# Moving the modulation weights, reordering the first loads and spreading the last adding DMAs in a one-core transformer pass

## Chip, cores and metric

One core of one Trainium2 chip. The metric is the time of one execution on the device in microseconds (us), a median over executions. The kernel before took 3865.44 us (two runs, 3865.24 to 3865.64).

## What is computed

One layer over 1152 tokens (128 of context, 1024 of samples) of width 1024, cut here to what the change touches:

```python
mod = silu(cond) @ w_mod + b_mod            # shift1, scale1, gate1, shift2, scale2, gate2, each 1024 wide
h   = x * (1 + scale1) + shift1             # context and sample tokens have each their own mod
z   = h @ w_in                              # 1024 -> 1728 columns
# mixer A: gelu, standardize, 128x128 spatial gate; mixer B: latent attention with 128 cached keys
x   = LN1(alpha * x + gate1 * (concat(A, B) @ w_o))
h2  = x * (1 + scale2) + shift2
# PEER: 8 heads x 16 experts of 16384 per token, by top-k of product keys
x   = LN2(alpha * x + gate2 * sum_k g_k * gelu(h2 . u[e_k]) * v[e_k])
```

## The kernel before, in words

Tokens are nine tiles of 128, tile 0 the context. Four blocks run one after the other; each ends when all engines have come to its end.

1. **mixer_inputs** (L149). First the shift1 and scale1 of both conditions: the table `w_mod` is read in 16 pieces of 128x1024 into four buffers in `free` (SP, L222), and TensorE takes each 128x128 piece as the stationary operand and two columns of `silu` as the moving one (L486: 16 pieces x 8 = 128 matmuls; an f32 matmul stands in the trace as two records). VectorE adds the bias (L325) and 1 (L328, `mod_ready`). The weights `w_in`, `w_s`, ... come by ScalarE's DMA queue (L380 to L384), and one semaphore, `wl`, stands for them all. GpSimd then zeroes the 25 MB table `g_cells` in 32 writes (L243), once `mod_ready` is there. Then, tile by tile: ScalarE makes the modulated rows (`mod_h`, L338) from `xt`, TensorE projects (`project`, L430) and does the rest of the tile (`finish`, L439 to L473), VectorE does `dve_tile`, ScalarE `act_tile` (gelu L345, evictions L361 to L373). `finish(i)` comes after `project(i+1)`; `mod_h(i+2)` stands in `act_tile(i)` ahead of the eviction L361 that frees TensorE for the transposes L468. `xt` is one buffer, loaded by SP at L225; the rotation table `rot` is one buffer too, loaded at L227. SP's order is: wait until `xt` has been read, load rows i, wait until the queries of tile i-1 are rotated (`qr_ready`), load table i.
2. **middle** (L506). Attention, output product, first LayerNorm, routing. Here shift2, scale2 and the gates are made in the other way: `silu` is the stationary operand (two columns of weights), a 128x512 piece of the table moves (`mod`, L715), the 2x512 result is copied to a row buffer `mrow` whose third row is the bias, and small matmuls against `sel` turn the row to columns (L727). For three of the sample tiles (3, 4, 5 are `DENSE[0]`; 0, 1, 2 are `DENSE[1]`; 6, 7, 8 `STILES`) the experts' weights go to dense tables. For `DENSE[1]` GpSimd adds them to `g_cells` by indirect DMAs of 128 cells, one for each of 128 (head, expert) columns and each of three tiles: 384 of them (`place`, L142), in 24 groups of 16. Groups of one tile are ordered by a wait at the head of each (L139). 20 of the 24 groups stand in this block.
3. **weigh** (L1201). TensorE, VectorE and ScalarE build the table `g_blocks` for `DENSE[0]`, SP stores it (L1230), and GpSimd issues the last 4 groups, 64 adding DMAs (L1239).
4. **experts** (L1347), the sweep. All 128 tiles of 128 experts are passed over twice (g = 0 to 255), first for `DENSE[0]`, then for `DENSE[1]`. TensorE does `hidden(g+2)` (L1511) and `down(g)` (L1525) in each step; SP loads `uw` (L1432) and `vw` (L1426) and every fourth step `gw`. Beside it GpSimd gathers rows for `STILES` (L1476, 384 gathers of 1 MB, two in four of five steps, into a ring of six, each after the VectorE sum `v_done` that frees its place), and VectorE does the dot products (L1613) and the sums (L1630). The second pass reads `g_cells` and waits for all adding DMAs; at g = 112 SP waits for those of the last tile too, as it overwrites `slots`.

Of the kernel before, what the change touches and what calls it, by code (L numbers as in the profile page):

```python
# [22 lines left out]
P = 128  # L23
# [77 lines left out]
def build(nc, a):  # L101
# [11 lines left out]
    with es:  # L113
# [10 lines left out]
        with ExitStack() as mid:  # L124
# [4 lines left out]
            mixer_inputs(nc, a, sb, sem, PS, ident, modc, sp1, silu, slots, krT, kT, vv, g_dram)  # L129
            placed = [sem(f"g_placed{d}") for d in range(CT)]  # L130
            middle(nc, a, sb, sem, PS, ident, modc, sp1, silu, slots, krT, kT, vv, x1_dram, gate_dram, g_dram, placed)
        weigh(nc, a, sb, sem, PS, ident, slots, g_dram, placed)
# [16 lines left out]
def mixer_inputs(nc, a, sb, sem, PS, ident, modc, sp1, silu, slots, krT, kT, vv, g_dram):  # L149

    with ExitStack() as c:
# [34 lines left out]
        NJ, NW = 2 * DK, 4  # L186
        free = sb(c, "free", [P, NW * D])
        bmod = sb(c, "bmod", [P, NJ])
        flat = slots[:, :, :].rearrange("p n c -> p (n c)")
        wm = free[:, 0:NW * D].rearrange("p (w k c) -> p w k c", w=NW, k=DK)  # L190
        hT1 = free[:, 0:D].rearrange("p (k t) -> p k t", k=DK)
        hs = [hT[:, :, :], hT1]
        zero = free[:, 2 * D:2 * D + ZW]
# [4 lines left out]
        ml = [sem(f"a_m{k}") for k in range(NW)]  # L198
        silu_ready, m_used, m_made, mod_ready, id0, id1 = (sem(f"a_{n}") for n in (
            "silu", "mused", "mmade", "mod", "id0", "id1"))  # L200
        xl, rl = sem("a_x"), sem("a_rot")
# [8 lines left out]
        nw = 12  # L210

        with nc.Block() as block:
            @block.sync
            def _(sp):
                sp.dma_start(cond[:, :, :], a["cond"]).then_inc(cl, 16)
                sp.dma_start(bmod[:, :], a["b_mod"]).then_inc(cl, 16)
                sp.dma_start(xt[:, :, :], a["xT"][0, :, :, :]).then_inc(xl, 16)
                sp.dma_start(rot[:, :, :], a["rot"][0, :, :, :]).then_inc(rl, 16)
                with sp.Fori(0, NJ // NW) as j:
                    for k in range(NW):  # L220
                        sp.wait_ge(m_used, j * NW + k + 1)
                        sp.dma_start(wm[:, k, :, :], a["w_mod"][j * NW + k, :, :, :]).then_inc(ml[k], 16)  # L222
# [98 lines left out]
            def _(dve):  # L321
                dve.wait_ge(cl, 32)
# [1467 lines left out]
```

## Time and profile before

| | |
|---|---|
| median of the runs | 3865.44 us |
| the profiled execution, own time | 3864.64 us |
| its span in the trace | 3862.8 us |
| mixer_inputs | 0 to 520.5 us |
| middle | 520.5 to 1459.3 us |
| weigh | 1459.3 to 1666.0 us |
| experts | 1666.0 us to the end |
| DVE busy, share of the span | 68% |
| ACT, POOL busy | 33%, 35% |

The trace gives each engine's instructions with start and length, and for idle time before them what ended it. PE is TensorE's matmul side, PEld its weight loads, DVE VectorE, ACT ScalarE, POOL GpSimd, SP the engine that issues most DMAs; "SPq" is an instruction in its queue. A row "[9.85 <-ACT ...]" says that the engine stood idle for 9.85 us until that instruction. In windows, PEclk is the granted clock as a share of 2.4 GHz, and the DMA share is the mean busy share of the 16 DMA engines.

### The profile page before, as it was taken

Reading aid. Unit: us, or ns where it says so; the run is one execution under the profiler, and the core shown is the slowest. Engines: PE = TensorE matmul, PEld = TensorE weight load, DVE = VectorE, ACT = ScalarE, POOL = GpSimd, SP = SyncE. Lnnn points to the kernel's source line nnn. Section 1 sums busy time; section 2 is a strip of 40 time slices with the busy share of each in tenths; the row PEclk is TensorE's granted clock in tenths of the full one; section 3 lists DMA queues with packets and bytes.
Section 4 is the critical chain, followed back from the end, with each engine's and each line's share of the span. In section 5 each row is a group of like instructions: output and inputs, shape, how many; then the busy total and the mean of one; then the engine's idle time right before and its main releaser. Section 6 shows DMA issues by size and latency. Waiting matters only on the chain.

```text
span 3862.8 us, 47329 instructions
## 1 busy us (share of the span) xinstructions
PE 3453.0 (89%) x17472; PEld 2853.2 (74%) x17472; DVE 2639.6 (68%) x5338; ACT 1273.8 (33%) x2399; POOL 1350.3 (35%) x828
## 2 busy tenths in 40 slices
PE   7877789999999976469999999999999999999996
PEld 6444434666666665459999999998888999999996
DVE  0111111566666699558888888888999888888866
ACT  0122222222322327523333333333333333333332
POOL 0100000078888847932322322332233223222302
PEclk9888889999999998879999999999999999999998
DMA  6500043355555544479999999999889998999953
GB/s 241 229 12 12 12 171 146 144 145 146 147 147 146 147 149 131 131 273 353 348 354 361 338 361 356 346 361 348 338 344 341 358 356 341 358 360 341 356 203 117
DMA packets 268027, 952.87 MB, mean 247 GB/s; under 512 B 74520, under 2 KB 125848, under 8 KB 208928
## 3 DMA queue, kind: packets, MB, share of 16 engines
q1 hardware_dynamic: 150720, 511.85, 36.0%
q0 software_dynamic: 115200, 428.07, 32.1%
q10 hardware_dynamic: 1888, 10.06, 0.6%
q8 instruction: 134, 2.20, 0.2%
q14 instruction: 85, 0.70, 0.1%
HBM read 888.70 MB, written 61.18 MB: 246 GB/s over the span
## 4 chain that ended last, share of the span: by engine, by line
PE 51%; DVE 4%; DMA 1%; issue 1%; ACT 0%; POOLq 0%; POOL 0%; SPq 0%; ACTq 0%; DVEq 0%
PE bank L1511 26%; PE bank L1525 25%; DMA vw<-in_v 1%; DVE ring L1613 1%; DVE accS L1630 1%; DVE uL L1691 1%; DVE vL L1686 0%; DVE slots L1668 0%; ACT vR L1576 0%; DVE st L1659 0%; DVE ga L1706 0%; DVE cL L1683 0%; DVE slots L1642 0%; DVE slots L1656 0%; DVE hL L1605 0%
## 5 line engine op out<-in xcount | busy, mean ns | idle before, releaser
L1476 POOL DMA_INDIRECT ring<-in_uv,slots x384 | 591.0, 1539 | 1396.9 <-DVE accS L1630 1301.0
L142 POOL DMA_INDIRECT g_cells<-slots x384 | 689.6, 1796 | 390.8 <-DVE slots L1178 263.8
L1511 PE MATMUL bank<-hR,uR 128*128 128x384 f32 x2048 | 692.1, 338 | 89.5 <-DVE uL L1691 89.5
L1511 PE MATMUL bank<-hR,uL 128*128 128x384 f32 x2048 | 691.6, 338 | 0.0
L1511 PE MATMUL bank<-hL,uR 128*128 128x384 f32 x2048 | 690.1, 337 | 0.0
L1630 DVE SCALAR_TENSOR_TENSOR accS<-ring,cs,accS 128x1024 f32<-128x1024 f32 x381 | 489.6, 1285 | 13.6
L1525 PE MATMUL bank<-vR,cR 128*128 128x512 f32 x1536 | 477.5, 392 | 0.7 <-DVE slots L1642 0.7
L1525 PE MATMUL bank<-vR,cL 128*128 128x512 f32 x1536 | 476.0, 391 | 0.0
L1525 PE MATMUL bank<-vL,cR 128*128 128x512 f32 x1536 | 475.7, 391 | 0.0
L1511 PEld LDWEIGHTS bank<-hR,uR 128*128 128x128 f32 x2048 | 388.0, 189 | 102.2 <-DVE uL L1691 92.6
L1613 DVE CUSTOM_DVE_ANT_0 ring<-ring,slots 128x1024 f32<-128x1024 f32 x384 | 460.2, 1236 | 0.1
L1570 ACT ACTIVATE cR<-ga 128x384 fp32r<-128x384 f32 x256 | 134.5, 525 | 924.9 <-PE bank L1525 829.1
L1511 PEld LDWEIGHTS bank<-hL,uR 128*128 128x128 f32 x2048 | 387.8, 189 | 9.6
L1511 PEld LDWEIGHTS bank<-hR,uL 128*128 128x128 f32 x2048 | 387.4, 189 | 0.0
L1686 DVE TENSOR_TENSOR vL<-vw,vR 128x1024 fp32r<-128x1024 f32 x256 | 319.9, 1250 | 60.3 <-ACT vR L1576 59.5
L1525 PEld LDWEIGHTS bank<-vL,cR 128*128 128x128 f32 x1536 | 288.3, 188 | 64.4
L1525 PEld LDWEIGHTS bank<-vR,cL 128*128 128x128 f32 x1536 | 288.2, 188 | 62.8
L1525 PEld LDWEIGHTS bank<-vR,cR 128*128 128x128 f32 x1536 | 284.7, 188 | 44.2 <-issue 1.0
L1691 DVE TENSOR_TENSOR uL<-uw,uR 128x1024 fp32r<-128x1024 f32 x256 | 311.9, 1218 | 5.6 <-ACT uR L1584 5.6
L1576 ACT ACTIVATE vR<-vw 128x1024 fp32r<-128x1024 f32 x256 | 267.7, 1046 | 18.5 <-DMA vw<-in_v 18.5
L771 PE MATMUL bank<-slots,wr 128*128 128x128 f32 x2304 | 264.2, 276 | 8.0 <-ACT slots L909 6.7
L1584 ACT ACTIVATE uR<-uw 128x1024 fp32r<-128x1024 f32 x256 | 267.6, 1045 | 6.3 <-DMA uw<-in_u 6.3
(226 smaller groups left out, 4048.3 us busy)
## 6 DMA issues: line engine op xcount, KB each, us to landing
uw<-in_u SPq DMA_DIRECT2D x256, 512.0 KB, 6.0
vw<-in_v SPq DMA_DIRECT2D x256, 512.0 KB, 6.9
wr<-in_w_pq SPq DMA_DIRECT2D x36, 2048.0 KB
wr<-in_w_o SPq DMA_DIRECT2D x18, 2048.0 KB
g_cells<-free POOLq DMA_DIRECT2D x32, 768.0 KB, 7.7
g_blocks<-stage SPq DMA_DIRECT2D x12, 2048.0 KB, 6.5
gw<-g_blocks SPq DMA_DIRECT2D x32, 768.0 KB, 13.8
gw<-g_cells SPq DMA_DIRECT2D x32, 768.0 KB, 8.8
```

The source lines that it names most:

```text
L142: pool.indirect_dma_start(out=g_dram[1][:, :], out_offset=bass.IndirectOffsetOnAxis(ap=slots[:, i, D + k:D + k + 1].bitcast(U32), axis=0), ...
L771: mm = pe.matmul(ps[:, l * P:(l + 1) * P], w[:, at:at + P], slots[:, i, k * P:(k + 1) * P], start=(k == 0), stop=(k == DK - 1))
L1476: pool.indirect_dma_start(out=ring[:, k % R, :], out_offset=None, in_=a["uv"], in_offset=bass.IndirectOffsetOnAxis(ap=ids[:, k // P, k % P ...
L1511: mm = pe.matmul(A[t][:, 0:CW], w[:, t, k, :], h[:, k, :], start=(k == 0 and w is uR and h is hR), stop=(k == DK - 1 and w is uL))
L1525: mm = pe.matmul(ACC[2 * tt + half][:, :], w[:, t, tt * P:(tt + 1) * P], v[:, t, half * 512:(half + 1) * 512], start=(m == 0 and w is cR a ...
L1570: act.activation(cR[:, x % 2, :], ga[:, x % 2, :], ACT.Copy).then_inc(c_r, 1)
L1576: act.activation(vR[:, x % 2, :], vw[:, x % 2, :], ACT.Copy).then_inc(v_r, 1)
L1584: act.activation(uR[:, x % 2, :, :], uw[:, x % 2, :, :], ACT.Copy).then_inc(u_r, 1)
L1613: dve.tensor_tensor_reduce(out=ring[:, k % R, 0:D], in0=ring[:, k % R, 0:D], in1=whole(STILES[k // P]), scale=1.0, scalar=0.0, op0=ALU.mul ...
L1630: dve.scalar_tensor_tensor(accS[:, t, :], ring[:, k % R, D:2 * D], one, accS[:, t, :], ALU.mult, ALU.add).then_inc(v_done, 1)
L1686: dve.tensor_tensor(vL[:, x % 2, :], vw[:, x % 2, :], vR[:, x % 2, :].bitcast(F32), ALU.subtract).then_inc(v_l, 1)
L1691: dve.tensor_tensor(uL[:, x % 2, :, :], uw[:, x % 2, :, :], uR[:, x % 2, :, :].bitcast(F32), ALU.subtract).then_inc(u_l, 1)
```

## The change

Four edits.

- **Modulation by moving weights.** shift1 and scale1 are now made as the block middle makes the rest: four pieces of 128x4096 (`wm`, lying in `big` and `slots`, which are free then), `silu` stationary with two columns, 4 x 8 matmuls of 512 columns, copy of each 2x512 row by VectorE, small matmuls against `sel_a` into columns.
- **First loads in one queue.** All first loads are issued by SP, in the order of use; ScalarE issues none. `w_in` comes in the four column groups of the projection, each with its semaphore (`zl`), the cached keys' weights have theirs (`kl`), the rest is waited for only ahead of `finish(0)`. Rows of tile 1 go straight into `hT1`, and are modulated in place.
- **Rows ahead of the rotation table.** SP's loop loads rows i, then waits for the queries of tile i-2 and loads table i-1.
- **Last adding DMAs in the sweep.** `place` takes a part of a group; the last 64 adding DMAs leave `weigh` and stand in `experts`, one in each of the steps g = 0 to 63, behind the step's gathers.

```diff
@@ place
-def place(pool, slots, g_dram, placed, d, h):
+def place(pool, slots, g_dram, placed, d, h, first=0, last=TOPK):
-    if h:
+    if h and first == 0:
         pool.wait_ge(placed[d], h * TOPK * 16)
-    for k in range(h * TOPK, (h + 1) * TOPK):
+    for k in range(h * TOPK + first, h * TOPK + last):
@@ mixer_inputs, sync
+                for ch in range(NM):
+                    sp.dma_start(wm[ch], a["w_mod"][ch, :, :]).then_inc(ml[ch], 16)
                 sp.dma_start(xt[:, :, :], a["xT"][0, :, :, :]).then_inc(xl, 16)
+                sp.dma_start(hT1, a["xT"][1, :, :, :]).then_inc(x1l, 16)
...
+                for n, (at, w) in enumerate(Z):
+                    sp.dma_start(w_in[:, :, at:at + w], a["w_in"][:, :, at:at + w]).then_inc(zl[n], 16)
...
-                with sp.Fori(1, NT) as i:
+                with sp.Fori(2, NT) as i:
                     sp.wait_ge(h_ready, i)
                     sp.dma_start(xt[:, :, :], a["xT"][i, :, :, :]).then_inc(xl, 16)
-                    sp.wait_ge(qr_ready, i)
-                    sp.dma_start(rot[:, :, :], a["rot"][i, :, :, :]).then_inc(rl, 16)
+                    sp.wait_ge(qr_ready, i - 1)
+                    sp.dma_start(rot[:, :, :], a["rot"][i - 1, :, :, :]).then_inc(rl, 16)
+                sp.wait_ge(qr_ready, NT - 1)
+                sp.dma_start(rot[:, :, :], a["rot"][NT - 1, :, :, :]).then_inc(rl, 16)
@@ mixer_inputs, tensor
+                def columns(ch):
+                    pe.wait_ge(m_row, ch + 1)
+                    for k in range(4):
+                        at = 8 * ch + 2 * k
+                        mm = pe.matmul(PS[7][:, at:at + 2], mrow[0:3, ch, k * P:(k + 1) * P], sel[:, :],
+                                       start=True, stop=True)
+                    mm.then_inc(m_cols, 1)
+
+                for ch in range(NM):
+                    pe.wait_ge(ml[ch], 16)
+                    for k in range(DK):
+                        mm = pe.matmul(PS[ch][0:2, :], silu[:, k, :], wm[ch][:, k * 512:(k + 1) * 512],
+                                       start=(k == 0), stop=(k == DK - 1))
+                    mm.then_inc(m_used, 1)
+                    if ch:
+                        columns(ch - 1)
+                columns(NM - 1)
+                pe.wait_ge(kl, 48)
                 pe.wait_ge(mod_ready, 1)
@@ weigh, gpsimd
-                for d, h in GROUPS[EARLY:]:
-                    place(pool, slots, g_dram, placed, d, h)
@@ experts, gpsimd
+                late = GROUPS[EARLY:]
...
+                    if g // TOPK < len(late):
+                        place(pool, slots, g_dram, placed, *late[g // TOPK], g % TOPK, g % TOPK + 1)
```

SP's queue at the start of mixer_inputs, before (the loop at L219 runs four times, the one at L223 eight times):

```order
L215 DMA cond<-in_cond 128x16
L216 DMA bmod<-in_b_mod 128x16
L217 DMA xt<-in_xT 128x1024
L218 DMA rot<-in_rot 128x128
...
L225 ISA [waits a_h]
L225 DMA xt<-in_xT 128x1024
L227 ISA [waits a_qr]
L227 DMA rot<-in_rot 128x128
```

And now (the loop at L234 runs seven times):

```order
L217 DMA cond<-in_cond 128x16
L218 DMA free<-in_b_mod 1x2048
L220 DMA big<-in_w_mod 128x4096 x2
L220 DMA slots<-in_w_mod 128x4096 x2
L221 DMA xt<-in_xT 128x1024
L222 DMA free<-in_xT 128x1024
L224 DMA w_kn<-in_w_kn 128x1024
L224 DMA cckT<-in_cckT 128x256
L224 DMA w_v<-in_w_v 128x1024
L226 DMA w_in<-in_w_in 128x8x512 x2
L226 DMA w_in<-in_w_in 128x8x384
L226 DMA w_in<-in_w_in 128x8x320
```

The pair of row load and table load looks alike in both loops; what has moved is the number of the tile that the table's wait (`a_qr`) asks for, one less than before against the rows loaded beside it, so that rows i no longer stand behind the rotated queries of tile i-2. The first loads stand in one line, the modulation table ahead of everything large.

GpSimd at the end of weigh and the start of the sweep, before (`ring` is the gathers' buffer, `g_cells` the table that the adding DMAs write):

```order
L1236 IOTA iob 128x128
L142 DMA g_cells<-slots 6291456x1 x64
L1224 UNCONDITIONAL_BRANCH
L1471 UNCONDITIONAL_BRANCH
L1476 DMA ring<-in_uv,slots 128x2048 x216
```

And now:

```order
L1260 IOTA iob 128x128
L1248 UNCONDITIONAL_BRANCH
L1493 UNCONDITIONAL_BRANCH
L1498 DMA ring<-in_uv,slots 128x2048 x8
L142 DMA g_cells<-slots 6291456x1 x2
L1498 DMA ring<-in_uv,slots 128x2048 x2
L142 DMA g_cells<-slots 6291456x1
L1498 DMA ring<-in_uv,slots 128x2048 x2
L142 DMA g_cells<-slots 6291456x1
```

The 64 adding DMAs have left the block weigh; eight gathers come first, then one or two adding DMAs between pairs of gathers.

## Rows read from the trace of the kernel before

**Rows 1.** The page's first part: busy time by engine, share of the span.

```profile
PE 3453.0 (89%) x17472; PEld 2853.2 (74%) x17472; DVE 2639.6 (68%) x5338; ACT 1273.8 (33%) x2399; POOL 1350.3 (35%) x828
```

**Rows 2.** Waits of PE in 120 to 500 us: total us, times, longest.

```profile
PE bank L468 <- ACT slots L361: 70.8, 7, 12.2
PE bank L430 <- ACT u L345: 20.1, 7, 4.5
```

**Rows 3.** Timeline of the start: start us, us, engine, line, operation.

```profile
26.93 54.77 PE L486 MATMUL bank<-silu,free 128*128 128x2 f32 x256 [26.93 <-DMA free<-in_w_mod]
...
82.04 0.17 DVE L328 TENSOR_SCALAR sp<-modc 128x16 f32<-128x16 f32 x1
```

**Rows 4.** Timeline: end of tile 0, projection, end of tile 1, projection.

```profile
143.06 1.46 PE L463 MATMUL bank<-w_qr,qlT 128*128 128x256 f32 x6
...
157.62 0.63 PE L473 MATMUL bank<-ident,qr 128*128 128x128 f32 x2
...
162.80 26.38 PE L430 MATMUL bank<-w_in,hT 128*128 128x512 f32 x64 [4.55 <-ACT u L345]
...
197.61 1.46 PE L463 MATMUL bank<-w_qr,qlT 128*128 128x256 f32 x6
...
201.78 0.33 SPq L225 DMA_DIRECT2D xt<-in_xT  x1
...
208.92 1.11 PE L468 MATMUL bank<-ident,u 128*128 128x128 f32 x4 [9.85 <-ACT slots L361]
...
209.83 0.63 PE L473 MATMUL bank<-ident,qr 128*128 128x128 f32 x2
...
213.09 25.12 PE L430 MATMUL bank<-w_in,free 128*128 128x512 f32 x64 [2.62 <-ACT u L345]
```

**Rows 5.** Timeline of PE: end of tile 7, which has no rows to wait for.

```profile
494.65 1.46 PE L463 MATMUL bank<-w_qr,qlT 128*128 128x256 f32 x6
495.95 0.60 PE L468 MATMUL bank<-ident,u 128*128 128x128 f32 x4
497.87 0.44 PE L473 MATMUL bank<-ident,qr 128*128 128x128 f32 x2 [1.32 <-DVE qr L318]
```

**Rows 6.** Windows: stretch, us, busy by engine, PEclk, DMA share, GB/s.

```profile
95.00:145.00 50.00, 48.92 (x177) 28.96 (x175) 6.97 (x30) 8.24 (x17) 13.29 (x25) 1.00 1.01 408
499.00:500.00 1.00, 0.00 (x0) 0.00 (x0) 0.00 (x0) 1.00 (x1) 0.00 (x0) 0.90 0.20 58
530.00:535.00 5.00, 5.00 (x9) 0.77 (x7) 0.00 (x0) 0.00 (x0) 0.00 (x0) 0.61 1.00 418
1611.00:1631.00 20.00, 0.00 (x0) 0.00 (x0) 0.00 (x0) 0.00 (x0) 16.07 (x11) 0.50 0.23 0
1700.00:2100.00 400.00, 400.00 (x2026) 364.31 (x2025) 351.64 (x464) 143.75 (x232) 116.86 (x76) 1.00 0.94 352
```

**Rows 7.** Timeline of the block middle's start: moving weights and their load.

```profile
520.50 0.34 SPq L644 DMA_DIRECT2D wr<-in_w_mod  x1
...
528.15 16.75 PE L715 MATMUL bank<-wr,silu 128*2 128x512 f32 x32 [3.73 <-DMA wr<-in_w_mod]
...
565.61 1.05 PE L727 MATMUL bank<-sel,s 3*128 3x2 f32 x8
...
568.04 7.03 PE L715 MATMUL bank<-wr,silu 128*2 128x512 f32 x16
```

**Rows 8.** Timeline in the second half of weigh: the 33rd of its 64 adding DMAs.

```profile
1545.76 56.59 POOL L142 DMA_INDIRECT g_cells<-slots  x1 [5.28 <-DMA g_cells<-slots]
```

**Rows 9.** Waits of SP in 1600 to 1850 us: total us, times, longest.

```profile
SPq L1224 <- PEq L1224: 55.4, 1, 55.4
```

**Rows 10.** The sweep: a gather, a later dot product (timelines); line L1476, 1700:2100, landing.

```profile
1711.50 1.86 POOL L1476 DMA_INDIRECT ring<-in_uv,slots  x1 [12.34 <-DVE accS L1630]
...
1729.55 1.22 DVE L1613 CUSTOM_DVE_ANT_0 ring<-ring,slots 128x1024 f32<-128x1024 f32 x1
...
DMA to landing us min/median/max: 6.5/9.5/12.2
```

More of the change, by code:

```diff
@@ L184, in mixer_inputs @@
         rs = sb(c, "rs", [P, G + 2])
-        NJ, NW = 2 * DK, 4
-        free = sb(c, "free", [P, NW * D])
-        bmod = sb(c, "bmod", [P, NJ])
+        NJ, NM = 2 * DK, 4
+        free = sb(c, "free", [P, 3 * D])
+        sel = sb(c, "sel_a", [3, 2])
         flat = slots[:, :, :].rearrange("p n c -> p (n c)")
-        wm = free[:, 0:NW * D].rearrange("p (w k c) -> p w k c", w=NW, k=DK)
+        wm = [tile[:, k * DK * 512:(k + 1) * DK * 512] for tile in (big, flat) for k in range(2)]
         hT1 = free[:, 0:D].rearrange("p (k t) -> p k t", k=DK)
+        mrow = free[0:3, D:3 * D].rearrange("p (c d) -> p c d", c=NM)
         hs = [hT[:, :, :], hT1]
-        zero = free[:, 2 * D:2 * D + ZW]
+        zero = free[:, D:D + ZW]
         zeroed = [sem(f"a_zero{k}") for k in range(4)]
@@ L197, in mixer_inputs @@
         cl, wl = sem("a_small"), sem("a_weights")
[L198 to L201, printed above, removed]
+        ml = [sem(f"a_m{k}") for k in range(NM)]
+        kl, zl = sem("a_kv"), [sem(f"a_in{n}") for n in range(len(Z))]
+        silu_ready, m_used, m_row, m_cols, m_made, mod_ready, sel_ready, id0, id1 = (sem(f"a_{n}") for n in (
+            "silu", "mused", "mrow", "mcols", "mmade", "mod", "sel", "id0", "id1"))
+        xl, x1l, rl = sem("a_x"), sem("a_xone"), sem("a_rot")
         h_ready, z_ready = sem("a_h"), sem("a_z")
@@ L377, in _ @@
             def _(act):
-                for dst, src in ((w_in, "w_in"), (w_s, "w_s"), (w_qn, "w_qn"), (w_qr, "w_qr"),
-                                 (w_kn, "w_kn"), (w_v, "w_v"), (cckT, "cckT")):
-                    act.dma_start(dst[:, :, :], a[src]).then_inc(wl, 16)
-                for dst, src in ((b_s, "b_s"), (g_q, "g_q"), (g_kv, "g_kv")):
-                    act.dma_start(dst[:, :], a[src]).then_inc(wl, 16)
-                for half in range(2):
-                    act.dma_start(krT[half * ROPE:(half + 1) * ROPE, P:2 * P], a["ckrT"]).then_inc(wl, 16)
                 act.wait_ge(cl, 32)
@@ L387, in _ @@
                 act.wait_ge(mod_ready, 1)
-                mod_h(act, 0, 0, 0)
-                mod_h(act, 1, 1, 1)
+                mod_h(act, 0, 0, 0, first=True)
+                act.wait_ge(x1l, 16)
+                mod_h(act, 1, 1, 1, src=hT1)
                 act.wait_ge(k_mm, 1)
@@ L428, in project @@
                         pe.wait_ge(lat_ready, i)
+                    if first:
+                        pe.wait_ge(zl[n], 16)
                     for k in range(DK):
@@ L492, in _ @@
                 values(pe, cckT)
-                project(pe, 0, 0)
+                project(pe, 0, 0, first=True)
                 project(pe, 1, 1)
+                pe.wait_ge(wl, nw * 16)
                 finish(pe, 0)
```

63 lines of the change are left out of this document (31 added, 32 removed).

## Prediction

> **What bounds the kernel now.** I read the page first. TensorE is busy for 89% of the span [rows 1], so what it does not do is 410 us, and a change that leaves its long stages alone can win only what stands in those gaps or what TensorE does needlessly. I then went through the gaps stage by stage.
>
> In the sweep there is nothing to win for a change that leaves its matmuls alone: in a stretch of 400 us TensorE is busy for 400 [rows 6]. The waits of TensorE in mixer_inputs name one cause: seven times, 70.8 us in all, it stands ahead of the transposes L468 until ScalarE has done the eviction L361 [rows 2]. The timeline says why. SP issues the rows at 201.78, behind the rotation of tile 1's queries, and ScalarE, which has the modulation of those rows ahead of its eviction, lets TensorE go on at 208.92 [rows 4]. Tile 7, whose ScalarE program has no modulation, has no such wait [rows 5]. Third, the start: TensorE waits until 26.93 and then needs 54.77 us for 256 records of two columns; the modulation is ready at 82.2 [rows 3]. Fourth, the end of weigh: SP has seen its last store land and then stands 55.4 us at the block's end [rows 9], with only GpSimd at work: its 33rd adding DMA had taken 56.59 us, to 1602.35 [rows 8], and 31 were still to come.
>
> **The start.** Removed: the 16 small pieces, and the wait behind ScalarE's loads. Added: four pieces of 2 MB, 32 matmuls of 512 columns. The block middle does just this. Its first piece is issued at 520.50 and TensorE starts on it at 528.15, 7.65 us later; a piece costs 7.03 us for 16 records [rows 7]. Here the first piece is issued behind two small loads, at about 1.7, so TensorE starts at 9.3. Next pieces come each 2.1 MB / 418 GB/s = 5.0 us later, the rate of SP's queue alone [rows 6], so TensorE is the slower one. Turning a row to columns costs 1.05 us for 8 records [rows 7], four times. 9.3 + 4 x 7.0 + 4 x 1.05 = 41.5, less some overlap of starts (each record group's length holds its pipeline fill), plus VectorE's copy and add, some 0.4: I take 41 for mod_ready against 82.2. Gain **41**. If TensorE starts at half its clock, as in the block middle (32 records in 16.75 us where two times 7.03 would be 14.06 [rows 7]), it is 38; if the copies to rows are all hidden and the first piece comes sooner, 44.
>
> The projection needs `w_in` by then. Ahead of it in the queue are 10.6 MB, at 418 GB/s landed at 28; `w_in`'s 7.1 MB take 17 more, 45. Its first part is needed at about 47 and its last at 66. Even at half that rate the last would come at 64. So this costs nothing, though the zeroing now begins while loads are under way. That zeroing fills the DMA engines (408 GB/s, share 1.01, for its whole length [rows 6]); it will end near 112, while tile 0's work ends near 106, and there ScalarE waits for two small stores. I put 2 us on that; 0 to 6 are possible.
>
> **The rows.** Rows i are now issued one tile earlier, and have some 45 us to land. What comes late next? Tile 7 shows it: from the start of L463 to the end of L473 it takes 498.31 - 494.65 = 3.66 us, with a new wait of 1.32 for VectorE's rotation [rows 5]; tile 1 takes 210.46 - 197.61 = 12.85 [rows 4]. Six tiles: the waits are 70.8 - 12.2 = 58.6 [rows 2], less 6 x 1.32, plus 6 x 0.7 for transposes that then run at the full clock (1.11 and 0.63 against 0.60 and 0.44 [rows 4, 5]): 54.9. Tile 0: 143.06 to 158.25 is 15.2 [rows 4]; its queries are copied, not rotated, so I leave it 2.5: 12.7, less the 2 for stores. Gain **65.6**. The wait of the next projection for ScalarE's gelu, 2.62 in tile 1, stays.
>
> **The clock.** The projection behind each gap takes 25.12 us in tile 1 [rows 4]; behind tile 0 it takes 26.38. By the 7.03 us that 8 x 512 columns take [rows 7], its 8 x 1728 would take 23.7. The rest is a start at 1.2 GHz after TensorE's pause. Will that go? In tile 7 the clock falls inside 499 to 500 [rows 6], 3.3 us after L468's end, although L473 ran between. The new gap from L468 to the projection is 1.32 + 0.44 + 2.6 = 4.4 us, as long as that. So the clock will fall in part of the tiles. Bounds: nothing, and 7 times the mean of 1.4 and 2.7 = 14. I take somewhat under 1 a tile, **6**, in the middle.
>
> **The adding DMAs.** With GpSimd out of weigh the 55.4 us of SP's wait go [rows 9], but for the engines' meeting itself; gain **55**. The work of weigh doesn't change. In the sweep each of steps 0 to 63 gets one more DMA on GpSimd. GpSimd is busy there for 116.86 of 400 us [rows 6], and 64 adds at some 1.5 (16.07 / 11 [rows 6]) to 2.4 us find room behind the gathers. On the DMA engines ten to eleven of them alone make a share of 0.23 in 20 us [rows 6]: 0.43 us of all sixteen each, or 5% of a step of the sweep, on top of 0.94 (a step is 42 records, 24 of L1511 and 18 of L1525, so the 2026 records of those 400 us [rows 6] are 48 steps of 8.3 us). That is close to full. Bounds: nothing, and 64 x 0.43 = 27 us if each pushes a load that TensorE waits for. TensorE waits for none in that stretch now, so I take **3** lost.
>
> By the Trainium skill (SBUF — State Buffer, Who interferes with whom) a VectorE instruction with two SBUF inputs contends with a GpSimd instruction that reads SBUF, and the second to issue is blocked until the first ends. The one 56.59 us instruction [rows 8] stands beside a VectorE that has such instructions back to back, and lasts much longer than any one of them; so the rule's direction agrees and its length doesn't.
>
> **Sum.** 41 + 65.6 + 6 + 55 - 3 = 164.6. The profiled execution took 3864.64 (span 3862.8 and 1.8 around it), 0.8 under the median: 3864.6 - 164.6 = **3700**.
>
> **Rivals.**
> - *The adding DMAs are held in the sweep, as one was in weigh.* VectorE is busy for 351.64 of 400 us [rows 6], so it pauses for 5 of the 41.5 us of five steps, mostly in the fifth, which has no dot products. An add that is held to that pause holds the gathers behind it, since GpSimd takes them in order. A gather is issued at 1711.50 for a dot product at 1729.55 and needs 9.5 to land [rows 10]: 8.5 us of slack. An add that is held through three steps (about 23 us) costs VectorE 14.5; in 64 / 5 = 12.8 such runs that is 185 us: 3700 + 185 = **3885**, slower than before. It decides from a net loss of 165 / 12.8 = 13 us in each run. Against it: in that stretch 76 instructions of GpSimd keep to 116.86 us, 1.54 each [rows 6], and they are of the same kind.
> - *A DMA-bound first pass.* The whole 27 us above, and loads that jitter more: **3725 to 3735**. For it: share 0.94 already.
> - *The rows come no earlier, or TensorE's wait only moves to another instruction of ScalarE.* Then the 65.6 and the 6 stay: **3771**. Against it: tile 7's row.
> - *The clock stays up in all tiles.* 8 us more on the clock, and 4 at the start if it is up there too: **3688**.
>
> **Chances.** Forecast 0.62; clock stays up 0.14; DMA-bound 0.14; rows no earlier, or weigh's end held by something else, 0.07; adds held 0.03. The forecast's own range is 3688 to 3714 (start -3/+3, stores -2/+4, clock -8/+6, sweep -3/+7, added as if independent and rounded up). To hold 8 in 10 I go to 3684 and 3728. A measurement tells about 2%, 77 us, from no change: the forecast is at 4.3%, so faster 0.95; the case of held adds, whole or in part, mostly lies within 2%: same 0.04, slower 0.01.
>
> **What would show it.** Right: mod_ready near 41; mixer_inputs ends near 408 to 416 instead of 520; no wait for an eviction ahead of the transposes; the sweep starts about 10 us after VectorE ends weigh; the first pass keeps steps of 8.31 us. Wrong: an adding DMA in the sweep over 5 us with dot products waiting for `ring`; TensorE waiting for VectorE's `uL` or `vL` in steps 0 to 63; waits for `zl` in tile 0; gelu L345 of tile 1 waiting much over 2 us for the small stores. The prediction as a whole is wrong if the sweep is longer by over 25 us than 2197, or the mixers' gain is under 90.

## The result, and the profile after

The changed kernel takes 3718.27 us (3717.35 to 3719.2) against 3865.44: ratio 0.9619, 95% interval 0.9578 to 0.9661. Run again beside the experiments it took 3716.55 (3716.06 to 3718.13), ratio 0.9616 (0.96 to 0.9632). The forecast was 3700, range 3684 to 3728: the sign and the range hold, and the sum is 18 us too favourable.

I first put the two profiled executions side by side by block, since that tells which terms to look at.

| stage | before, us | after, us | difference | forecast |
|---|---|---|---|---|
| start, to `mod_ready` | 82.2 | 44.1 | -38.1 | -41 |
| rest of mixer_inputs | 438.3 | 380.4 | -57.9 | -71.6 |
| middle | 938.8 | 938.6 | -0.2 | 0 |
| weigh | 206.7 | 151.0 | -55.7 | -55 |
| experts | 2196.8 | 2203.3 | +6.5 | +3 |
| span | 3862.8 | 3717.4 | -145.4 | -164.6 |

The page's first part, against [rows 1]. TensorE's busy time falls by 22 us (for the most part the two columns' matmuls), GpSimd's by 46 (the one long adding DMA).

```profile
PE 3430.8 (92%) x17312; PEld 2805.9 (75%) x17312; DVE 2640.8 (71%) x5343; ACT 1277.7 (34%) x2399; POOL 1304.7 (35%) x828
```

**The start**, a timeline as in [rows 3]. TensorE starts at 9.44 instead of 26.93. Its first 32 records take 16.48 us, where two times 7.03 [rows 7] would be 14.06; the last rows are the modulation's columns, VectorE's copy, and the add that is `mod_ready`. SP stands 30.20 us at its own issues of `w_in`, with nothing urgent behind.

```profile
6.28 30.20 SPq L226 DMA_DIRECT2D w_in<-in_w_in  x4
...
9.44 16.48 PE L506 MATMUL bank<-big,silu 128*2 128x512 f32 x32 [9.44 <-DMA big<-in_w_mod]
...
41.73 1.94 PE L499 MATMUL bank<-sel_a,free 3*128 3x2 f32 x16
...
43.70 0.19 DVE L342 COPY modc<-bank 128x32 f32<-128x32 f32 x1 [1.19 <-PE bank L499]
43.93 0.17 DVE L344 TENSOR_SCALAR sp<-modc 128x16 f32<-128x16 f32 x1
```

**The tiles**, TensorE's waits from 90 to 424 us, against [rows 2]. The 70.8 us for the eviction are gone. In their place stand eight waits of 1.32 for the rotated queries, as tile 7 had foretold [rows 5], and one for gelu is now 12.3 long.

```profile
PE bank L443 <- ACT u L362: 27.7, 7, 12.3
PE bank L486 <- DVE qr L331: 10.6, 8, 1.3
```

The timeline around that one wait, and the next two projections. ScalarE issues the two small stores of tile 0 and stands 9.90 us until they have landed; its gelu, and with it TensorE's projection of tile 2, come behind. The projections take 25.8 and 26.2 us, where [rows 4] has 26.38 and 25.12.

```profile
106.95 0.39 ACTq L409 DMA_DIRECT2D out_new_ckv<-ckv  x1
107.37 1.25 ACTq L410 DMA_DIRECT2D out_new_krope<-kr  x1
117.23 1.28 ACT L362 ACT_TABLE_LOAD   x1 [9.90 <-DMA out_new_krope<-kr]
...
119.18 25.80 PE L443 MATMUL bank<-w_in,hT 128*128 128x512 f32 x64 [12.27 <-ACT u L362]
...
159.63 26.04 PE L443 MATMUL bank<-w_in,free 128*128 128x512 f32 x64 [2.57 <-ACT u L362]
200.33 26.18 PE L443 MATMUL bank<-w_in,hT 128*128 128x512 f32 x64 [2.58 <-ACT u L362]
```

The windows (columns as in [rows 6]) say why the stores are slow: to 112 us the DMA engines are full, by the zeroing.

```profile
106.00:112.00 6.00, 0.83 (x6) 0.35 (x4) 0.41 (x1) 0.90 (x2) 0.53 (x1) 0.85 1.03 410
112.00:114.00 2.00, 0.00 (x0) 0.00 (x0) 0.00 (x0) 0.00 (x0) 0.00 (x0) 0.50 0.96 282
```

**The end of weigh.** SP's wait of 55.4 us [rows 9] is 0.2.

```profile
SPq L1248 <- PEq L1248: 0.2, 1, 0.2
```

**The adds in the sweep**, the answer for line L142 (ns: shortest, median, longest), and a window of 400 us among them, against the last of [rows 6]. No add is held for long. GpSimd's busy time goes from 116.86 to 215.83 us, the DMA share from 0.94 to 0.97, and TensorE does not notice: 400.00 of 400.

```profile
L142 POOL DMA_INDIRECT g_cells<-slots x64: 1607/1978/2416, 1549.0 to 2070.8; - x64
```

```profile
1550.00:1950.00 400.00, 400.00 (x2024) 364.17 (x2023) 351.83 (x465) 144.60 (x232) 215.83 (x125) 1.00 0.97 352
```

Of the 19 us that the sum is too favourable, 13.7 are missing in the tiles, in two terms (the rows and the clock); the start is 2.9 short, and the sweep has lost 6.5 us at a place still to be found.

### The profile page after: what moved, and what is told of

Read it like the earlier page. It is cut to its first block, busy times and chain, and to the rows that moved or that the text cites. A ratio compares the mean times of both kernels' runs of the same rounds, so it can differ in the third digit from the quotient of the medians.

```text
span 3717.4 us, 46918 instructions
## 1 busy us (share of the span) xinstructions
PE 3430.8 (92%) x17312; PEld 2805.9 (75%) x17312; DVE 2640.8 (71%) x5343; ACT 1277.7 (34%) x2399; POOL 1304.7 (35%) x828
## 4 chain that ended last, share of the span: by engine, by line
PE 51%; DVE 5%; DMA 2%; issue 1%; ACT 0%; SPq 0%; POOLq 0%; POOL 0%; ACTq 0%; DVEq 0%
PE bank L1536 26%; PE bank L1550 25%; DMA vw<-in_v 2%; DVE ring L1638 1%; DVE accS L1655 1%; DVE uL L1716 1%; DVE vL L1711 1%; DVE cL L1708 0%; DVE ga L1731 0%; DVE slots L1693 0%; ACT vR L1601 0%; DVE slots L1667 0%; DVE st L1684 0%; DVE slots L1681 0%; DVE hL L1630 0%
## 5 line engine op out<-in xcount | busy, mean ns | idle before, releaser
L142 POOL DMA_INDIRECT g_cells<-slots x384 | 642.9, 1674 | 386.3 <-DVE slots L1202 263.9
L1550 PEld LDWEIGHTS bank<-vR,cR 128*128 128x128 f32 x1536 | 284.7, 188 | 44.1 <-issue 0.9
L1708 DVE TENSOR_TENSOR cL<-ga,cR 128x384 fp32r<-128x384 f32 x256 | 149.5, 584 | 171.3 <-ACT cR L1595 122.5
```

The lines of the kernel that those rows point to most:

```text
L142: pool.indirect_dma_start(out=g_dram[1][:, :], out_offset=bass.IndirectOffsetOnAxis(ap=slots[:, i, D + k:D + k + 1].bitcast(U32), axis=0), ...
L1550: mm = pe.matmul(ACC[2 * tt + half][:, :], w[:, t, tt * P:(tt + 1) * P], v[:, t, half * 512:(half + 1) * 512], start=(m == 0 and w is cR a ...
L1708: dve.tensor_tensor(cL[:, x % 2, :], ga[:, x % 2, :], cR[:, x % 2, :].bitcast(F32), ALU.subtract).then_inc(c_l, 1)
```

## The experiments

Every kernel is timed against the one before on the same chip. That one took 3865.56 us beside the first four kernels, 3867.92 beside the four of the store stall, the clock and ScalarE's loads ahead of its silu, and 3867.15 beside the other four. A difference of two kernels from different groups is therefore known to about 2.5 us only; where it is small, the blocks' starts in the profiles are given too. The four that leave a part of the change out, or do it alone, come first, then the misses.

### The change again

> The changed kernel, once more. If the sweep's 6.5 us over before (2203.3 against 2196.8 us, with three loads of vw that took 12 to 24 us near step 112 where before had one) belong to the change, this profile has them again, with the sweep at 2203 +/- 1 and the time at 3718. If they are the chance of one execution, the sweep lies between 2196 and 2204 and the times spread by some us.

Measured: 3716.55 (3716.06 to 3718.13). The gain is a property of the two programs, and the experiments below are set against both figures of the change, 3716.55 and 3718.27.

### Only the adding DMAs moved

```diff
@@ before: place, weigh, experts as in the change; mixer_inputs untouched
```

> Before, with the adding DMAs of weigh in the sweep and nothing else. Theory (weigh was held by GpSimd alone, the sweep hides the adds): weigh 151 us instead of 206.7, first pass with steps of 8.31 us, so 3865 - 55 + 0 to 6 = 3810 to 3816. Rival (the adds are what makes the sweep 6.5 us longer): 3816, with TensorE's late steps near step 112 as in the changed kernel. If the sweep is 2197 here, the 6.5 us come from elsewhere and it is 3810.

Measured: 3810.72 (3808.02 to 3812.04), ratio 0.9857 (0.984 to 0.9873): 54.8 us gained, where the forecast had 55 less 3. The waits of TensorE ahead of the transposes stay (69.3 us). The longest of its 64 adds in the sweep takes 2.60 us.

### The change without that part

```diff
@@ weigh, gpsimd
+                for d, h in GROUPS[EARLY:]:
+                    place(pool, slots, g_dram, placed, d, h)
@@ experts, gpsimd
-                    if g // TOPK < len(late):
-                        place(pool, slots, g_dram, placed, *late[g // TOPK], g % TOPK, g % TOPK + 1)
```

> The changed kernel with the 64 adding DMAs back in weigh. Theory: +50 to +56 us, 3768 to 3774. In before one add there took 56.6 us beside a VectorE that paused nowhere. If such a hold is a matter of chance in the order of the two engines, weigh is shorter here or has its hold elsewhere: 64 adds at 2.7 us apiece end after 175 us, so weigh could be 175 to 207 us and the time 3742 to 3774. If it is fixed by the program, weigh is 206.7 again.

Measured: 3774.29 (3770.51 to 3775.85), ratio 0.9762: 57.7 us are given back. The long add is there again, and SP's wait with it, as in [rows 8] and [rows 9]:

```profile
1450.44 56.63 POOL L142 DMA_INDIRECT g_cells<-slots  x1 [5.25 <-DMA g_cells<-slots]
```

```profile
SPq L1248 <- PEq L1248: 55.3, 1, 55.3
```

56.63 against 56.59: what holds it belongs to the program at that place, not to the chance of one execution. Both traces also show what the hold ends with. Here is VectorE's last instruction of weigh in the kernel before, and then in this one with the add that follows the long one:

```profile
1600.39 0.54 DVE L1342 TENSOR_TENSOR cb<-e,wf 128x384 f32<-128x384 bf16 x1
```

```profile
1505.07 0.58 DVE L1366 TENSOR_TENSOR cb<-e,wf 128x384 f32<-128x384 bf16 x1
...
1507.37 1.54 POOL L142 DMA_INDIRECT g_cells<-slots  x1 [0.30 <-issue]
```

VectorE ran without a pause beside the long add, up to 1600.93 and 1505.65; the add ended at 1602.35 and 1507.07, 1.42 us later both times, which is nearly the length of an add beside an idle VectorE (1.54). So the add seems to have got hardly anywhere until VectorE stopped. Most of the adds shortly ahead of it took 2.43 beside the same VectorE work. That VectorE holds it is argued from these rows; no kernel changed VectorE's work there, and why the 33rd is held and the 32nd is not stays open (the 33rd is the first in this block behind a wait of GpSimd for its own DMAs, 5.28 and 5.25 us). Moving the adds took them away from that place.

### The change with the rows in their old place

```diff
@@ mixer_inputs, sync
+                sp.wait_ge(qr_ready, 1)
+                sp.dma_start(rot[:, :, :], a["rot"][1, :, :, :]).then_inc(rl, 16)
                 with sp.Fori(2, NT) as i:
                     sp.wait_ge(h_ready, i)
                     sp.dma_start(xt[:, :, :], a["xT"][i, :, :, :]).then_inc(xl, 16)
-                    sp.wait_ge(qr_ready, i - 1)
-                    sp.dma_start(rot[:, :, :], a["rot"][i - 1, :, :, :]).then_inc(rl, 16)
-                sp.wait_ge(qr_ready, NT - 1)
-                sp.dma_start(rot[:, :, :], a["rot"][NT - 1, :, :, :]).then_inc(rl, 16)
+                    sp.wait_ge(qr_ready, i)
+                    sp.dma_start(rot[:, :, :], a["rot"][i, :, :, :]).then_inc(rl, 16)
```

> The changed kernel with SP's old order (rows i behind the rotated queries of tile i-1). Theory: TensorE waits again ahead of the transposes in tiles 0 to 6, 9.8 us each less the 1.3 us that stand there now, 6 x 8.5 + 8 to 11 for tile 0; the stall for the small stores in tile 0 is partly the same time, so +52 to +62: 3770 to 3780. Rival (the clock's behaviour gives some of it back): the projections start at the half clock in both orders, so this adds under 3 us either way.

Measured: 3773.53 (3772.06 to 3775.28), ratio 0.9761: the order of two DMAs on SP is worth 57 us. Its waits of TensorE from 90 to 480 us are those of [rows 2] again:

```profile
PE bank L481 <- ACT slots L378: 71.4, 7, 13.2
```

### The first modulation with weights at rest, in the new queue

The changed kernel, with the 16 pieces as stationary operand as before (128 matmuls, bias added by VectorE), from the four new loads.

```diff
@@ mixer_inputs, tensor
-                    for k in range(DK):
-                        mm = pe.matmul(PS[ch][0:2, :], silu[:, k, :], wm[ch][:, k * 512:(k + 1) * 512],
-                                       start=(k == 0), stop=(k == DK - 1))
+                    for q in range(4):
+                        for k in range(DK):
+                            mm = pe.matmul(acc[:, 4 * ch + q, :], wm[ch][:, k * 512 + q * P:k * 512 + (q + 1) * P],
+                                           silu[:, k, :], start=(k == 0), stop=(k == DK - 1))
```

> The changed kernel with the first modulation by weights that stay in the array and two columns that move, as before (128 matmuls in 16 pieces, bias added by VectorE), but with the one queue and its order kept. Theory A (moving the weights is worth what TensorE spends on the form: 54.8 us before against 30.6 here): TensorE from 9.4 to about 64 us, mod_ready at 64 to 66 us against 44.1, the projections' weights are there by then, so the first tile goes by 20 us later and all after it: 3733 to 3740. Theory B (the form was paced by its loads in two queues, and with one queue the weights at rest take about as long as moving ones): 3714 to 3722. The old 54.8 us had no stated wait inside, so I take A, 3737.

Measured: 3735.77 (3734.42 to 3736.88), ratio 0.966. TensorE starts at 9.5 and `mod_ready` is at 64.79 (its row: 64.62, 0.17 long), 20.7 us later than in the changed kernel; the time is 17.5 to 19.2 longer. Theory A. So of the start's 38.1 us about 20 belong to the form of the matmul and the rest, 17.5 (26.93 less 9.44), to the loads: their order, their queues and the size of the pieces (2 MB here too, 0.5 MB before). The next two ask about the queues.

### Two queues, ScalarE's loads ahead of its silu

```diff
@@ mixer_inputs: the loads of w_kn, cckT, w_v, w_in, b_s, ... ckrT move from sync to scalar
             def _(act):
+                for dst, src in ((w_kn, "w_kn"), (cckT, "cckT"), (w_v, "w_v")):
+                    act.dma_start(dst[:, :, :], a[src]).then_inc(kl, 16)
+                for n, (at, w) in enumerate(Z):
+                    act.dma_start(w_in[:, :, at:at + w], a["w_in"][:, :, at:at + w]).then_inc(zl[n], 16)
...
                 act.wait_ge(cl, 32)
                 act.activation(silu[:, :, :], cond[:, :, :], ACT.Silu).then_inc(silu_ready, 1)
```

> The changed kernel with the weights' first loads issued by ScalarE again, ahead of its silu, beside SP's queue. Theory: ScalarE is held by its queue and makes silu near 21 us or later, and the modulation's pieces share the DMA engines with 8 MB of other weights; mod_ready near 22.5 + 4 x 7 + 4 = 54 to 58 instead of 44, so +10 to +14 us, 3728 to 3732. Then the single queue is worth 10 to 14 of the 38 us at the start and the moving weights the rest. Rival (the single queue is what matters): +25 us or more.

Measured: 3755.08 (3749.36 to 3759.72), ratio 0.9703: 37 to 39 us lost, three times what was expected. By its figure this is the rival's case (the single queue is what matters), but the cause is narrower than that. The timeline of ScalarE shows a thing that I had not priced. Its queue stands 33.93 us at the four issues of `w_in`, and the silu waits behind them:

```profile
2.18 33.93 ACTq L388 DMA_DIRECT2D w_in<-in_w_in  x4
36.14 4.07 ACTq L390 DMA_DIRECT2D b_s<-in_b_s  x1
...
45.64 0.21 ACT L396 ACTIVATE silu<-cond 128x16 f32<-128x16 f32 x1
```

### Two queues, the silu first

The same, with the two lines of the silu ahead of the loads.

> The changed kernel, with the weights' loads issued by ScalarE as in the run with two queues (3755.1), but behind its silu instead of ahead of it. Theory A (what cost 37 us there is that ScalarE stood at its own DMA issues, 33.9 us at w_in, with the silu behind them): the silu is done by 10 us, TensorE starts at 9 to 12 us, and what is left is that w_mod shares the DMA engines: at half of 408 GB/s its four chunks of 2 MB land about 10 us apart instead of 5, TensorE's 30.6 us stretch to at most 45, mod_ready between 44 and 58 us, time 3716 to 3732. Theory B (the sharing of the DMA engines is what costs, wherever the silu stands): the last chunk of w_mod lands at 65 us or later, mod_ready near 80 as in the run before, time 3745 to 3758.

Measured: 3720.08 (3716.68 to 3725.41), ratio 0.9625 (0.9609 to 0.9641), which includes the changed kernel's 0.9616. Theory A at its favourable end: ScalarE stands as long, with nothing that TensorE needs behind it yet, and the sharing of the DMA engines costs 0.2 us at `mod_ready` (44.32 against 44.10).

```profile
2.98 0.21 ACT L386 ACTIVATE silu<-cond 128x16 f32<-128x16 f32 x1 [0.95 <-DMA free<-in_b_mod]
...
4.57 32.25 ACTq L390 DMA_DIRECT2D w_in<-in_w_in  x4
```

```profile
44.15 0.17 DVE L334 TENSOR_SCALAR sp<-modc 128x16 f32<-128x16 f32 x1
```

This also reads the kernel before anew. There, too, ScalarE's silu stood behind its loads, as its timeline shows: 12.35 us at one small issue, and the silu only at 22.38. TensorE's first row there names the DMA of `w_mod` at 26.93 [rows 3], the last of the things it waited for; that load shared the DMA engines with the weights. So there both were late, and which would have been enough alone no kernel tried.

```profile
6.07 12.35 ACTq L382 DMA_DIRECT2D g_kv<-in_g_kv  x1
...
22.38 0.21 ACT L386 ACTIVATE silu<-cond 128x16 f32<-128x16 f32 x1
```

The Trainium skill (Trainium Kernel Development and Optimization, Key Constraints) says that issuing from several engines saves no more than issue time, as all transfers share the same DMA engines. The run with the silu first agrees (44.32 against 44.10), and the one with the silu behind shows that the issue time is not small on an engine that has something else to do.

### The store stall: waited for later

ScalarE waits for the two stores ahead of tile 1's square root instead of ahead of its gelu.

```diff
@@ mixer_inputs, scalar
                 act.wait_ge(var_ready, i + 1)
+                if not first:
+                    act.wait_ge(stored, 32)
                 act.activation(sd[:, :], var[:, :], ACT.Sqrt).then_inc(sd_ready, 1)
...
                 act.dma_start(a["new_krope"], kr[:, 0, :]).then_inc(stored, 16)
-                act.wait_ge(stored, 32)
```

> The changed kernel, where ScalarE waits for the two small stores of tile 0 only ahead of tile 1's root (which lets VectorE overwrite their source), not ahead of tile 1's gelu. Theory (the projection of tile 2 waits 12.3 us because ScalarE stands for 9.9 us on these stores): that wait falls to 2.6, -9 to -10 us, 3708 to 3709. Rival (TensorE waits for something else as well): under -4 us.

Measured: 3712.29 (3710.24 to 3713.59), ratio 0.9597 (0.9581 to 0.9613): 4.3 us better. The longest wait of the projections is 3.9 instead of 12.3, while ScalarE now stands 6.02 us ahead of the square root. In the profiles the block middle begins at 417.3 us, against 424.5 and 423.4 in the two of the changed kernel, so 6.1 to 7.2 of the 8.4 come through in the tiles. The medians show less, and they come from two groups (6.6 us if each is set against its own kernel before). The 9 to 10 expected were too much either way.

### The store stall: zeroing behind the stores

```diff
@@ mixer_inputs, gpsimd
-                pool.wait_ge(mod_ready, 1)
+                pool.wait_ge(stored, 32)
                 pool.memset(zero, 0.0).then_inc(zero_set, 1)
```

> The changed kernel, where GpSimd zeroes g_cells only after the two small stores have landed. Theory (the stores are slow because the zeroing fills the DMA engines, and the changed kernel starts it 38 us earlier against less work ahead of the stores): they land in 2 to 3 us as in before, the wait of the projection falls from 12.3 to 4.6, -7 to -8 us, 3710 to 3711; nothing later needs the table before 740 us. If the stores are slow for another reason, 3718.

Measured: 3711.0 (3710.63 to 3713.13), ratio 0.9595 (0.9579 to 0.9611): 5.5 us better. ScalarE's stand falls from 9.90 to 4.01 and the projection's wait to 6.38, and the block middle begins 5.4 to 6.5 us earlier:

```profile
111.50 1.28 ACT L362 ACT_TABLE_LOAD   x1 [4.01 <-DMA out_new_krope<-kr]
...
113.45 25.42 PE L443 MATMUL bank<-w_in,hT 128*128 128x512 f32 x64 [6.38 <-ACT u L362]
```

With nothing but the time of the zeroing changed, the stores land 5.9 us sooner, so the zeroing is the cause of these 5.9 us. It is not the whole stall. In the kernel before, ScalarE stood only 2.12 us for the same two stores. In the changed kernel and in this one SP issues the next rows beside them (at 107.44 and 107.61); the DMA share from 108 to 110 us is 0.91 here, where the kernel before had 0.27 in the two microseconds behind its stores. No kernel moved these rows.

### The clock kept up

TensorE multiplies `ident` by `w_kn` in its pauses, into a bank whose content has been read by then; these results are unused.

```diff
@@ mixer_inputs, finish
                 mm.then_inc(tra, 1)
+                pe.wait_ge(v_ev, i + 2)
+                pe.matmul(PS[6][:, :], ident[:, :], w_kn[:, 0, :], start=True, stop=True)
+                pe.matmul(PS[6][:, 0:P], ident[:, :], w_kn[:, 0, 0:P], start=True, stop=True)
                 pe.wait_ge(qr_ready, i + 1)
...
                 mm.then_inc(trq, 1)
+                for w in (512, 512, 256):
+                    pe.matmul(PS[6][:, 0:w], ident[:, :], w_kn[:, 0, 0:w], start=True, stop=True)
```

> The changed kernel with five extra matmuls per tile, whose results nobody reads, in TensorE's two pauses at the end of a tile (640 columns in the first, 1280 in the second). Theory (each projection takes 26.2 us instead of 23.4 because the clock falls in those 4.4 us): clock at its upper level through the projections of tiles 3 to 8, 2.8 us less each, minus up to 0.5 us where the extra matmuls overrun: -14 to -17 us, 3701 to 3704. Rival (the projection is slow for its reads or waits): no gain or +3 us.

Measured: 3703.05 (3699.47 to 3710.75), ratio 0.957 (0.9554 to 0.9586): 13.5 us better. The profiled execution is the longest of the four. First the windows of the changed kernel at the pause between tile 1's end and the projection of tile 3 behind it, then those of this one:

```profile
158.00:159.00 1.00, 0.00 (x0) 0.00 (x0) 0.00 (x0) 0.99 (x2) 0.00 (x0) 0.52 0.49 142
161.00:163.00 2.00, 2.00 (x3) 0.67 (x2) 0.98 (x9) 1.97 (x5) 0.00 (x0) 0.50 0.00 0
```

```profile
158.00:159.00 1.00, 1.00 (x4) 0.39 (x3) 0.00 (x0) 1.00 (x1) 0.00 (x0) 1.00 0.30 78
161.00:163.00 2.00, 2.00 (x6) 0.89 (x5) 0.98 (x10) 1.97 (x5) 0.00 (x0) 1.00 0.03 8
```

PEclk is 1.00 through the pause instead of 0.50 (1.2 GHz), and the same two microseconds hold six records instead of three. The projections of tiles 3 to 8 take 23.44 to 23.47 us, near the 23.7 that the prediction had worked out for a full clock; only tile 2's, behind the store stall, keeps 25.92:

```profile
119.42 25.92 PE L443 MATMUL bank<-w_in,hT 128*128 128x512 f32 x64 [9.35 <-ACT u L362]
160.00 23.44 PE L443 MATMUL bank<-w_in,free 128*128 128x512 f32 x64 [0.42 <-ACT u L362]
198.11 23.47 PE L443 MATMUL bank<-w_in,hT 128*128 128x512 f32 x64 [0.43 <-ACT u L362]
```

There is a price that I had overlooked. The block middle, whose code is the same, takes 943.7 us here, against 938.5 to 938.8 in every profiled kernel without the added matmuls, so 5.1 of the 13.5 to 14.6 us that the tiles gain in this profile are given back. The clock shows where: the same work, 140 to 150 us into the block, in the changed kernel and then in this one:

```profile
564.50:574.50 10.00, 9.46 (x52) 6.19 (x53) 2.30 (x7) 3.41 (x11) 0.00 (x0) 1.00 0.02 7
```

```profile
549.89:559.89 10.00, 10.00 (x20) 4.40 (x20) 1.98 (x5) 0.83 (x3) 0.00 (x0) 0.50 0.00 1
```

A pause of TensorE at which the changed kernel keeps its clock (about 563 us) is one at which this kernel loses it (about 547). Why is not shown.

### The sweep's loss: late loads spread

At step 112 SP issues four loads of LayerNorm rows and gates together, 2 MB. They are put at steps 112, 114, 116 and 118.

```diff
@@ experts, sync
-                    if g == NEt - 16:
-                        sp.wait_ge(h_l, 2)
-                        sp.wait_ge(placed[2], PAIRS * 16)
+                    if NEt - 16 <= g < NEt - 8 and g % 2 == 0:
+                        if g == NEt - 16:
+                            sp.wait_ge(h_l, 2)
+                            sp.wait_ge(placed[2], PAIRS * 16)
+                        k_ln = (g - NEt + 16) // 2
...
-                                         (gate_1, gate_dram[1, :, :].rearrange("p (a b) -> p a b", a=4))):
+                                         (gate_1, gate_dram[1, :, :].rearrange("p (a b) -> p a b", a=4)))[k_ln:k_ln + 1]:
```

> The changed kernel with the four loads of layer norm rows and gates (2 MB) issued two steps apart, at steps 112, 114, 116 and 118 of the sweep, instead of all at step 112. Theory A (the late half of the sweep's 6.5 us is that these loads push three loads of weights past their time: 13.3, 11.9 and 23.5 us against one of 21.8 before): no wait of TensorE for weights over 6 us near step 112, time lower by 3 to 5 us: 3711 to 3714. Theory B (the sweep is bound by bandwidth there, and bytes moved later are waited for later): 3715 to 3718, unchanged.

Measured: 3708.23 (3705.07 to 3709.98), ratio 0.9588 (0.9572 to 0.9604): 8 to 10 us, more than the 3 to 5 expected. In the profiles the windows from 2400 to 2500 us (columns as in [rows 6]), of the changed kernel, then of this one, show most of it: TensorE is busy for 92.77 of 100 us, and here for all 100, with a DMA share of 1.01.

```profile
2400.00:2500.00 100.00, 92.77 (x459) 84.46 (x458) 81.39 (x108) 33.60 (x53) 28.48 (x18) 0.95 0.93 347
```

```profile
2400.00:2500.00 100.00, 100.00 (x507) 91.04 (x506) 91.58 (x122) 36.38 (x58) 31.72 (x21) 1.00 1.01 387
```

Is that loss the moved adds' doing, as I had thought? The sweep's length in the profiles, from VectorE's first `uL` to the end of the span, tells:

| kernel | adds in the sweep | sweep, us |
|---|---|---|
| before | no | 2192.0 |
| change, adds back in weigh | no | 2197.5 |
| only the adds moved | yes | 2195.9 |
| the change, two executions | yes | 2198.4, 2196.4 |
| silu first; store wait later | yes | 2195.9, 2198.6 |
| late loads spread | yes | 2188.3 |

With and without the adds the lengths overlap. The sweep of the change is 4 to 6 us longer than the one execution of before, whether the adds are in it or not. The profiles that the table leaves out agree: 2196.4 (rows in their old place), 2196.6 (zeroing later), 2198.6 (clock kept), 2198.7 (weights at rest), 2202.7 (two queues, silu behind), and 2186.3 with all four edits, which spread the late loads too.

### All four together

> The changed kernel with the four edits that cost nothing else: the store's wait moved to ahead of tile 1's square root (alone 4.3 us less), zeroing behind the stores (alone 5.5 less), the added matmuls in the projections' pauses, whose results nothing uses (alone 13.5 less), the late loads spread. The first two take away the same 10 us stand of ScalarE, so together 7 to 9 less; with them gone the clock is also kept up in tile 2 (25.9 to 23.5, 2.4 less). Sum: 3716.5 - 8 - 13.5 - 2.4 - 0 to 4 = 3688 to 3693. If the pauses that keep the clock down come back in another tile, or the edits overlap more: 3697 to 3703.

Measured: 3685.13 (3680.07 to 3692.19), ratio 0.9531 (0.9515 to 0.9547), against 0.9616 (0.96 to 0.9632) for the change. That is 3 us less than the 3688 to 3693 expected. All seven late projections are at the full clock now, tile 2's too, and the block middle is 943.7 us long again:

```profile
110.60 23.47 PE L444 MATMUL bank<-w_in,hT 128*128 128x512 f32 x64 [0.97 <-ACT u L362]
148.73 23.44 PE L444 MATMUL bank<-w_in,free 128*128 128x512 f32 x64 [0.42 <-ACT u L362]
```

This beats both kernels, and lies 180 us under the one before. The four edits alone gave 4.3, 5.5, 13.5 and 8.3 us against 3716.55, which is 31.6; together they give 31.4.

## Why the prediction was right, and where it was off

**The start (41, measured 38.1): mechanism and form right, the term 3 too large.** The step that failed is "4 x 7.0". The first 32 records took 16.48 instead of 14.06, like the first 32 in [rows 7] with 16.75; the prediction had named this (38) and chosen the other value. The rest is the columns' last turn and VectorE's copy. The account of what the order of the loads does was incomplete: "the wait behind ScalarE's loads" is also a silu held at ScalarE's own issues. In the changed kernel with the silu ahead, two queues are as good as one.

**The rows ahead (65.6, measured about 57 to 60).** The mechanism is shown by the kernel with the old order: 57 us, and the wait of 71 comes back. Tile 7's row gave the new wait of 1.32 to the hundredth. The term mis-sized is "2 us for the small stores", with 0 to 6 as its bounds: it is 7.7 (the projection's wait in tile 2, 12.27, against 4.55 in [rows 4]). The prediction had both facts, zeroing that fills the DMA engines to about 112 and stores issued at about 106, but did not add them: issued at 107 beside a full share of 1.03, the stores landed at 117.2, after that was over. The zeroing accounts for 5.9 us of ScalarE's stand, and the two kernels for the stall give back 4.3 and 5.5 us. The next rows, which now load beside the stores, were not in the prediction at all.

**The clock (6 gained, measured 2.4 lost): this step failed, in sign.** The seven projections take 183.1 us in place of 180.7. The step was "So the clock will fall in part of the tiles": it falls in all seven, and is 0.50 behind the new pause too. What the prediction also missed is that the old pauses differed in what they cost. The three short projections of before (25.1 to 25.2 us) had the clock back 3.4 to 3.6 us after their start, the four long ones (26.3 to 26.4) after 5.6 to 5.9. In the changed kernel it takes 4.7 to 5.8 us in all seven. The windows, 4 us after the start of the short projection of [rows 4], of the long one after it in the kernel before, and of tile 4's in the changed kernel:

```profile
217.00:218.00 1.00, 1.00 (x4) 0.52 (x3) 1.00 (x5) 0.00 (x0) 0.00 (x0) 1.00 0.00 0
266.00:267.00 1.00, 1.00 (x2) 0.34 (x1) 1.00 (x6) 0.00 (x0) 0.00 (x0) 0.50 0.00 0
```

```profile
204.00:205.00 1.00, 1.00 (x3) 0.48 (x2) 1.00 (x4) 1.00 (x4) 0.00 (x0) 0.50 0.00 0
```

So three short ones became long, 3.05 us lost together, and the four long ones gained 0.6. That the lost time is the clock is shown by the added matmuls (23.45 us each). Why every second projection of before recovered sooner stays open: the transposes and waits ahead of both kinds are the same to 0.1 us (from the transposes to the projection 4.17 and 4.08 us).

**The adding DMAs (55, measured 55.7; alone, 54.8).** Right in mechanism and size.

**The sweep (-3, measured -6.5).** Size near, cause wrong. The adds' share in it is not to be told from zero: 2197.5 us without them, 2198.4 and 2196.4 with them. The largest wait that an edit removed sits where SP issues 2 MB of loads at once (one of 6.3 to 8.5 us in every changed kernel, two of together 5.5 in the kernel before, none over 0.7 with the loads spread), and the cost is there in the kernel before too (95.25 of 100 us busy in its window from 2552 to 2652, as against 92.77). Why that window is 2.5 us worse in the changed kernels with unchanged sweep code stays open; the gather's and the loads' times relative to each other differ from run to run, and no kernel set them.

**The rivals.** The held adds (3885) and the DMA-bound first pass (3725 to 3735) fall: no add over 2.42 us, TensorE busy for 400.00 of 400. Rows no earlier (3771) falls. The kernel that does just this takes 3773.5, but that nearness is luck: the rival's price was 71.6 us and its base 3700, and the measured ones are 57 and 3716.6. The clock that stays up (3688) did not come of itself; forced, it gave 3703, and with the other three edits 3685. That the time came within the range owes something to the range: four of the sum's terms erred to the same side.

In sum: 164.6 less 2.9 (start), 5.7 (stores), 8.4 (clock), 3.5 (sweep), plus 0.7 (weigh) and 0.2 (middle) is 145.0, and the spans differ by 145.4; the rest is rounding.

## What to carry to other kernels

Where one engine issues DMAs for several consumers in a loop, look at what it waits for ahead of each issue: swapping a load past a wait it does not need was worth 57 us here, and the tile without the load had already shown the new schedule's waits. An engine that computes should issue its first small operation ahead of its large loads, since it may stand tens of microseconds at the issue. When a stage is pulled forward, list what now runs beside it: a 25 MB zeroing under two small stores cost more than anything else that the prediction missed, but for the clock.

## What the runs showed of the hardware that I had not expected

- The engine that issues the four column groups of `w_in` stands for 30.20 us (SP), 32.25 and 33.93 (ScalarE) at these issues, while the four loads of `w_mod`, of 2 MB each, went out of SP within some 2 us (1.59 to 3.7). In the kernel before, `w_in` as one load of the same 7.1 MB, first in its queue, went out of ScalarE in 0.42 us. Which property of the four does it, whether the shape of their pieces or how much is already queued, was not tried.
- One indirect adding DMA in weigh holds GpSimd for 56.59 and 56.63 us in two programs, always in the same place of the block, and ends 1.42 us behind the last of VectorE's unbroken row of instructions; the same DMAs in the sweep take 1.6 to 2.4 us (2.60 at most with only the adds moved) beside a VectorE that is busy for 351.83 of 400 us. The Trainium skill (SBUF — State Buffer, Who interferes with whom) has a GpSimd instruction blocked until the VectorE instruction ahead of it ends. The sweep's adds, at most 0.9 us longer than the 1.54 beside an idle VectorE, leave room for a hold of less than one instruction of 1.2 us; the one in weigh outlasts dozens of them.
- In the first microseconds the clock column is no guide. It shows 1.00 from 9 to 13 us (first row below), and five records fit into four microseconds there, where from 15 to 17 six fit into two.

```profile
9.00:13.00 4.00, 3.56 (x5) 0.62 (x6) 0.00 (x0) 0.00 (x0) 0.00 (x0) 1.00 1.00 426
...
15.00:17.00 2.00, 2.00 (x6) 0.43 (x5) 0.00 (x0) 0.00 (x0) 0.00 (x0) 1.00 0.99 426
```

- Matmuls whose results nothing reads, put into TensorE's pauses, paid 13.5 us: they took no time in the tiles, as TensorE waited there anyway, and kept the granted clock at 1.00. In both kernels that have them the block behind was 5.1 us longer, with the clock down in one more place.
